# Router logits taken inside the layer-norm stage, with the norm's gain folded into the router's weights; sums of squares and parameter loads placed one stage earlier

## The reference

```python
x = _layernorm(DEEPNORM_ALPHA * x + mix, ln1_g[l], ln1_b[l])
ffn = _hier_moe(x, router_group_w[l], router_group_b[l], router_expert_w[l], ...)
x = _layernorm(DEEPNORM_ALPHA * x + ffn, ln2_g[l], ln2_b[l])

def _layernorm(x, g, b):            # (x - mean) / sqrt(var + 1e-5) * g + b
def _hier_moe(x, wg, bg, we, be, w_gate, w_up, w_down):
    glog = x @ wg + bg              # 4 group logits of each token
    elog = x @ we + be              # 16 expert logits of each token
    # best group, its two best experts, their weights; the experts' outputs are summed
```

```python
def rmsnorm(x, w):  return x * rsqrt(mean(x * x) + 1e-6) * w
```

## Time and profile before

| | us |
|---|---|
| median of 3 runs (2122.65 to 2130.05) | 2123.17 |
| profiled execution | 2123.46 |
| its span in the trace | 2121.3 |
| PE busy | 1743.2 (82%) |
| DVE busy | 1164.8 (55%) |
| ACT busy | 878.9 (41%) |
| POOL busy | 662.5 (31%) |

### The profile page before, as it was taken

One profiled execution on the slowest core, in us unless ns is written; L12 is line 12 of the kernel. 1 busy time (PEld: TensorE's weight loads), 2 busy tenths in 40 slices (PEclk: granted clock), 3 DMA queues, 4 the chain that ended last, 5 costly groups with the idle time before them and its releaser, 6 DMA issues. The chain is left out here.

```text
span 2121.3 us, 22435 instructions
## 1 busy us (share of the span) xinstructions
PE 1743.2 (82%) x7978; PEld 1347.0 (63%) x7978; DVE 1164.8 (55%) x1693; ACT 878.9 (41%) x1294; POOL 662.5 (31%) x348
## 2 busy tenths in 40 slices
PE   5999995859991799997666995499697689999997
PEld 4876532647870686742555884388367477888885
DVE  3926565649975564645556995592466414143241
ACT  2246555127872235655314884322645322111111
POOL 2337523101110333731401120144352023444441
PEclk8999987859995999997767997799889899999998
DMA  4201111057963311020117994320000122222221
GB/s 174 80 32 40 40 40 59 1 223 299 371 252 150 117 70 42 1 66 14 60 40 291 359 380 180 120 100 23 17 3 1 60 99 100 99 94 87 96 79 49
DMA packets 40476, 233.83 MB, mean 110 GB/s; under 512 B 9316, under 2 KB 9700, under 8 KB 20660
## 3 DMA queue, kind: packets, MB, share of 16 engines
q1 hardware_dynamic: 31012, 215.42, 26.9%
q0 software_dynamic: 9216, 16.80, 2.2%
q10 hardware_dynamic: 144, 0.26, 0.0%
HBM read 226.00 MB, written 23.23 MB: 117 GB/s over the span
## 5 line engine op out<-in xcount | busy, mean ns | idle before, releaser
L256 PE MATMUL bank<-XS,WS 128*128 128x512 f32 x864 | 201.9, 396 | 22.3 <-DVE WS L381 20.8
L2213 POOL TENSOR_TENSOR WS<-ring,WS 128x2048 fp32r<-128x2048 f32 x31 | 149.5, 4822 | 190.7 <-ACT WS L2205 190.7
L256 PEld LDWEIGHTS bank<-XS,WS 128*128 128x128 f32 x864 | 165.4, 192 | 58.4 <-DVE WS L381 21.3
L1235 PE MATMUL bank<-WS,XS 128*128 128x512 f32 x768 | 187.3, 400 | 1.1 <-DVE XS L1355 1.1
L2234 PE MATMUL bank<-XS,WS 128*128 128x512 f32 x768 | 174.9, 389 | 3.0 <-DVEq L2263 3.0
L2252 PE MATMUL bank<-WS,US 128*128 128x512 f32 x768 | 174.7, 389 | 0.0
L2205 ACT CAST WS<-ring 128x2048 fp32r<-128x2048 f32 x31 | 59.2, 1911 | 271.7 <-PE bank L2234 144.1
L1235 PEld LDWEIGHTS bank<-WS,XS 128*128 128x128 f32 x768 | 145.2, 193 | 31.3 <-DVE XS L1355 1.9
L2234 PEld LDWEIGHTS bank<-XS,WS 128*128 128x128 f32 x768 | 144.1, 188 | 33.1 <-DVEq L2263 3.2
L2252 PEld LDWEIGHTS bank<-WS,US 128*128 128x128 f32 x768 | 144.1, 188 | 29.9
L1572 PE MATMUL bank<-XS,WS 128*128 128x512 f32 (+1 forms) x600 | 136.4, 389 | 2.7 <-POOLq L1623 2.7
(11 more groups left out here) (487 smaller groups left out, 3534.8 us busy)
## 6 DMA issues: line engine op xcount, KB each, us to landing
raw<-in_w_exp SPq DMA_DIRECT2D x16, 2048.0 KB, 13.4
DN<-in_w_exp SPq DMA_DIRECT2D x32, 1024.0 KB
ring<-in_w_ff SPq DMA_DIRECT2D x32, 1024.0 KB, 4.7
raw<-in_w_in SPq DMA_DIRECT2D x20, 1024.0 KB, 4.8
GU<-in_w_exp SPq DMA_DIRECT2D x8, 2048.0 KB, 15.7
XT<-in_w_exp SPq DMA_DIRECT2D x8, 2048.0 KB, 16.1
ring<-in_w_in SPq DMA_DIRECT2D x12, 1024.0 KB, 4.8
raw<-in_w_out SPq DMA_DIRECT2D x8, 1024.0 KB, 5.0
```

The source lines that it names most:

```text
L256: last = pe.matmul(m.ps[g % 8][:, :], WS[:, i % 2, hw, at:at + P], XS[:, hx, k, :], start=(step == 0), stop=(step == 3 * KD - 1))
L1235: last = pe.matmul(m.ps[2 + e % 2][:, :], r.XS[:, e % 2, hx, 4 * half + k, :], r.WS[:, half, hw, k * S:(k + 1) * S], start=(half == 0 and ...
L2213: pool.tensor_tensor(f.WS[:, q % 2, 1, :], f.ring[:, q % 4, :], f.WS[:, q % 2, 0, :].bitcast(F32), ALU.subtract).then_inc(w_low, 1)
```

## The change

The second `transpose_stage` of a layer is gone, and so are the 32 logit matmuls of `router`. Both are now part of `norm_stage`, which works on the standardised tile before gain and bias: PE transposes each tile (`turn`), ACT copies the two banks to XT (`home`), PE makes the tile's logits with the folded weights WG = gain times WR as the stationary and XT as the moving operand (`logits_of`), ACT copies the 20 rows (`logits_back`) and PE transposes them back (`route`). The norm's bias enters through a row WB that is added to RP. DVE's gain and bias on X (`finish`) now wait until the tile has been transposed. At the stage's start the first weight quarter is cast in two halves, ahead of the chunks, and its low part is DVE's.

In the layer's first stage SP issues one weight chunk, then the parameters, then the other three chunks. In the second block the sums of squares of tiles 0 to 2 are taken at the end of the stage ahead (`combine_norm`, `out_projection_2`, `feed_forward`), and only that of tile 3 is left in `rms_transpose` and `final_norm` (which has the same lines as the diff shows of `rms_transpose`); `feed_forward` has the lines of `out_projection_2` with `summed` at 37 + t.

```diff
 def transpose_stage(nc, m, XS=None, loads=None, params=None):
-                loads(sp)
+                loads(sp, (0,))
             if params:
                 n = params(sp, param_in)
+            if loads:
+                loads(sp, (1, 2, 3))
...
 def norm_stage(nc, m, ln, layer, XS, WS):
         @block.tensor
         def _(pe):
...
+            def turn(t):
+                for half in range(2):
+                    pe.wait_ge(standard, 2 * t + half + 1)
+                    for k in range(4):
+                        last = pe.transpose(m.ps[2 * t + half][:, k * P:(k + 1) * P], m.X[:, t, (4 * half + k) * P:(4 * half + k + 1) * P], m.ident[:, :])
+                    last.then_inc(turned, 1)
+            def logits_of(t):
+                for k in range(KD):
+                    if k % 4 == 0:
+                        pe.wait_ge(xt_home, 2 * t + k // 4 + 1)
+                    last = pe.matmul(m.ps[2 * t][0:20, 0:P], ln.WG[:, k, :], m.XT[:, k, t * P:(t + 1) * P], start=(k == 0), stop=(k == KD - 1))
+                last.then_inc(logits, 1)
+            def route(t):
+                pe.wait_ge(logits_home, t + 1)
+                pe.transpose(m.ps[1][:, t * 20:(t + 1) * 20], ln.LT[0:20, t * P:(t + 1) * P], m.ident[0:20, 0:20]).then_inc(routed, 1)
...
+                        for k in range(4):
+                            if k % 2 == 0:
+                                pe.wait_ge(first_low, k // 2 + 1)
+                            pe.wait_ge(xt_low, k + 1)
...
+            for t in range(NT):
+                for half in range(2):
+                    pe.wait_ge(w_low, 2 + half)
+                    product(1, t, half).then_inc(tile_done, 1)
+                if t >= 1:
+                    turn(t - 1)
+                if t >= 2:
+                    logits_of(t - 2)
+                if t >= 3:
+                    route(t - 3)
+            logits_of(2)
+            route(1)
+            turn(3)
+            route(2)
+            logits_of(3)
+            route(3)
...
+        @block.scalar
+        def _(act):
...
+            first(0)
+            high(0)
+            high(1)
+            first(1)
+            high(2)
+            high(3)
+            weights(1)
+            for k in range(4, KD):
+                high(k)
+            weights(2)
+            weights(3)
+            standardise(0)
+            standardise(1)
+            home(0)
+            standardise(2)
+            home(1)
+            logits_back(0)
+            standardise(3)
+            home(2)
+            logits_back(1)
+            logits_back(2)
+            home(3)
+            logits_back(3)
...
+        @block.gpsimd
+        def _(pool):
+            for q in range(1, 4):
+                pool.wait_ge(w_high, q)
+                if q == 2:
+                    pool.wait_ge(xt_low, KD)
+                pool.tensor_tensor(WS[:, q, 1, :], m.raw[:, q, :], WS[:, q, 0, :].bitcast(F32), ALU.subtract).then_inc(w_low, 1)
...
         @block.vector
         def _(dve):
...
             def finish(t):
-                dve.wait_ge(standard, t + 1)
+                dve.wait_ge(turned, 2 * t + 2)
...
 def router(nc, m, r):
-            for t in range(NT):
-                for k in range(KD):
-                    last = pe.matmul(m.ps[0][:, t * 20:(t + 1) * 20], m.XT[:, k, t * P:(t + 1) * P], m.WR[:, k, :],
-                                     start=(k == 0), stop=(k == KD - 1))
-            last.then_inc(logits_done, 1)
...
 def combine_norm(nc, m, ln, r, layer):
+            def square(t):
+                act.wait_ge(finished, t + 1)
+                act.activation(r.MIX[:, t, 0:D], m.X[:, t, :], ACT.Square, accum_out=m.SS[:, t:t + 1]).then_inc(squared, 1)
...
+                if t >= 2:
+                    square(t - 2)
+            square(NT - 2)
+            act.wait_ge(squared, NT - 1)
...
 def rms_transpose(nc, m, n, XS, gain, first, extra=None):
-            for t in range(NT):
-                act.activation(n.XN[:, t, :], m.X[:, t, :], ACT.Square, accum_out=n.SS[:, t:t + 1]).then_inc(act_step, 1)
-            act.wait_ge(act_step, NT)
+            act.activation(n.XN, m.X[:, NT - 1, :], ACT.Square, accum_out=m.SS[:, NT - 1:NT]).then_inc(act_step, 1)
+            act.wait_ge(act_step, 1)
...
 def out_projection_2(nc, m, f):
+            for t in range(NT - 1):
+                act.wait_ge(summed, NT + t + 1)
+                act.activation(f.XQ, m.X[:, t, :].rearrange("p (a n) -> p a n", a=2), ACT.Square, accum_out=m.SS[:, t:t + 1]).then_inc(squared, 1)
+                act.wait_ge(squared, t + 1)
...
 def build(nc, d, out):
...
                         norm_stage(nc, m, ln, layer, XS, WS)
-                    transpose_stage(nc, m)
```

More of the change, by code:

```diff
@@ L962, in _, with product @@
         def _(pe):
-            if XS:
-                for kh in range(2):
-                    pe.wait_ge(xt_low, 4 * (kh + 1))
-                    for n in range(2 * NT):
-                        half, t = (n % 2, n // 2) if kh else (n // NT, n % NT)
-                        pe.wait_ge(w_low, 2 * kh + half + 1)
+            def product(kh, t, half):
+                step = 0
+                for k in range(4):
+                    for hw, hx in TERMS:
+                        last = pe.matmul(m.ps[2 * t + half][:, :], XS[:, hx, 4 * kh + k, t * P:(t + 1) * P], WS[:, 2 * kh + half, hw, k * S:(k + 1) * S],
+                                         start=(kh == 0 and step == 0), stop=(kh == 1 and step == 11))
+                        step += 1
+                return last
@@ L972, in _ @@
                         for k in range(4):
+                            if k % 2 == 0:
+                                pe.wait_ge(first_low, k // 2 + 1)
+                            pe.wait_ge(xt_low, k + 1)
                             for hw, hx in TERMS:
-                                last = pe.matmul(m.ps[2 * t + half][:, :], XS[:, hx, 4 * kh + k, t * P:(t + 1) * P], WS[:, 2 * kh + half, hw, k * S:(k + 1) * S],
-                                                 start=(kh == 0 and step == 0), stop=(kh == 1 and step == 11))
+                                pe.matmul(m.ps[0][:, :], XS[:, hx, k, 0:P], WS[:, 0, hw, k * S:(k + 1) * S], start=(step == 0), stop=False)
@@ L976, in _ @@
                                 step += 1
-                        if kh:
-                            last.then_inc(tile_done, 1)
+                        continue
+                    if half:
+                        pe.wait_ge(w_low, 1)
+                    if half and t == NT - 1:
+                        pe.wait_ge(weights_ready, 2)
+                    product(0, t, half)
+            pe.wait_ge(xt_low, KD)
+            for t in range(NT):
+                for half in range(2):
+                    pe.wait_ge(w_low, 2 + half)
[6 more added lines that the diff above has]
+                    route(t - 3)
@@ L993, in finish @@
                 link(dve.tensor_tensor(m.X[:, t, :], m.X[:, t, :], ln.GB[:, D:2 * D], ALU.add))
+            link(dve.tensor_tensor(ln.WG[:, :, :], m.WR[:, :, :], column(C_LB), ALU.mult))
+            dve.reduce_sum(ln.WB[:, :], ln.WG[:, :, :].rearrange("p k n -> p n k"), AX.X).then_inc(weights_ready, 1)
+            first(0)
+            low(0)
+            low(1)
+            first(1)
+            low(2)
+            low(3)
+            dve.wait_ge(weights_ready, 1)
+            link(dve.tensor_tensor(ln.WG[:, :, :], m.WR[:, :, :], column(C_LG), ALU.mult))
+            dve.wait_ge(bias_sum, 1)
+            dve.tensor_tensor(m.RP[:, R_RB:R_RB + 20], m.RP[:, R_RB:R_RB + 20], m.ps[7][:, 0:20], ALU.add).then_inc(weights_ready, 1)
+            for k in range(4, KD):
+                low(k)
             for t in range(NT):
@@ L2094, in out_projection_2 @@
 def out_projection_2(nc, m, f):
-    names = ("raw_in", "first_low", "w_high", "w_low", "xt_high", "xt_low", "block_done", "tile_done", "summed")
-    with stage(nc, "out_projection_2", *names) as (block, (raw_in, first_low, w_high, w_low, xt_high, xt_low, block_done, tile_done, summed)):
+    names = ("raw_in", "first_low", "w_high", "w_low", "xt_high", "xt_low", "block_done", "tile_done", "summed", "squared")
+    with stage(nc, "out_projection_2", *names) as (block, (raw_in, first_low, w_high, w_low, xt_high, xt_low, block_done, tile_done, summed, squared)):
         ORDER = (1, 0, 3, 2)
@@ L2205, in _ @@
                 act.copy(f.WS[:, q % 2, 0, :], f.ring[:, q % 4, :]).then_inc(w_high, 1)
+            for t in range(NT - 1):
+                act.wait_ge(summed, 37 + t)
+                act.activation(f.SQ[:, :, :].rearrange("p a n -> p (a n)"), m.X[:, t, :], ACT.Square, accum_out=m.SS[:, t:t + 1]).then_inc(final_squared, 1)
+                act.wait_ge(final_squared, t + 1)
         @block.gpsimd
@@ L2370, in build, with first_loads @@
                 one = bass.ds(layer, 1)
[L2372 to L2373 removed]
+                def first_loads(sp, chunks):
+                    for i in chunks:
```

137 lines of the change are left out of this document (74 added, 63 removed).

## The result

| | before | after |
|---|---|---|
| median of 4 runs, us | 2123.81 (2122.65 to 2130.05) | 2068.35 (2061.51 to 2071.16) |
| profiled execution | 2123.46 | 2069.1 |
| its span | 2121.3 | 2067.4 |
| PE, DVE, ACT, POOL busy | 1743.2, 1164.8, 878.9, 662.5 | 1734.3, 1138.7, 890.2, 652.5 |

The medians are 55.5 us apart. The ratio is 0.9728, interval 0.9698 to 0.9759, which is a gain of 51 to 64 us. PE lost 9 us of busy time and DVE 26: most of the gain is waiting, which the busy times do not show. The prediction was 2062, range 2054 to 2076.

What follows compares the result with a forecast made beforehand. Time was taken as a sum of barrier-ended stages, each set by what ends last. Norm stage and router 44.6, parameters 10.4, squares 2.2, 3.1 and 0.9 sum to 61.2 us, so 2123.5 - 61.2 = 2062, range 2054 to 2076.

Steps and rivals of the forecast that it cites:

- Start of the norm stage: Norm stage's start: PE's first product 3.0 us after the stage's start instead of 8.7, 5.7 us gained a layer.
- Added to PE: Norm stage: eight transposes 1.03 us, 16 logit records 1.73; 3.8 us ahead of the last tile's products, last product at 407.2.
- The tail: Norm stage behind the last product: router's first DVE step at 418.1 instead of 440.43, 22.3 us a layer, 44.6 in all.
- What the removed part cost: Between norm stage and router's first step: nothing but transposing and logits from 418.21 to 440.43, 22.2 us, each layer.
- Router's next bound: Router: SP's write of X, 7 us in all, stays hidden by 5 us behind DVE's routing of 12.4 us.
- Parameters: Layers' first stages: parameters ahead of three chunks land some 7.5 us earlier, before DVE ends; gain 5.0 + 5.4 = 10.4 us.
- Rival 3: First stages: early parameters do not land early, as their rows share engines with the chunks; 10.4 lost, 2073 us; chance 0.11.
- Squares: Second block, three of four squares moved a stage ahead: first rms_transpose 2.2 us, second 3.1, final_norm 0.9.
- Rival 1: Norm stage's start: DVE's fourth low part falls behind POOL's first (margin 0.5 us), PE stands 3.3 us a layer, 2069; chance 0.17.
- Rival 2: Norm stage's tail runs at 1.2 GHz after PE's pause: 2.3 us more a layer, 2067; chance 0.12.
- Rival 4: Experts: folded weights push one expert over 128 tokens, another pass of some 200 us, kernel ends at 2260; chance 0.02.
- The sum: Whole kernel: 44.6 + 10.4 + 2.2 + 3.1 + 0.9 = 61.2 us gained, 2062; as summed, chance 0.55.

Runs made afterwards that it cites:

- tail: Changed kernel with ACT's home(2) placed ahead of standardise(3): 2063.59 us, ratio 0.9729.
- params_only: Kernel before with one edit, parameters issued behind the first weight chunk: 2113.89 us against 2125.04, ratio 0.9948.
- norm_only: Kernel before with the norm stage and router of the changed one, parameters and squares as before: 2088.57 us, ratio 0.9821.
- slip: Changed kernel with two spare subtractions on DVE ahead of the fourth chunk's low part, so POOL's first starts first: 2077.54 us, ratio 0.9775.

## Why the prediction was right, point by point

- *Start of the norm stage*, 5.7 a layer: right in the place (PE at 3.06, forecast 3.0). Undone with the rest in place, it was worth 4.7.
- *Added to PE*: turn 1.03 as forecast; logits_of 1.92 where 1.73 was taken, in 16 records of 0.12. Last product at 399.5 - 346.9 = 52.6 us after the start; forecast 407.2 - 354.9 = 52.3.
- *The tail*: forecast from the last product to the router's first step 418.1 - 407.2 = 10.9, measured 411.04 - 399.5 = 11.5. The chain was the right one, through ACT's order; `tail` showed it by taking 1.8 to 2.4 out of it. Sum for this part: 21.3 and 20.7 a layer for 22.3. The step that was mis-sized is the logits' duration, which is exposed twice behind the last product and once ahead, 0.6 in all; the rest of the 1.0 to 1.6 I put down to small hand-overs between PE and ACT that were taken as nothing; no run separates them.
- *What the removed part cost*: 22.2 us was read off as the price of transposing and logits. The prediction did not see that some 5.8 of it came from half clock. It made no difference to the forecast, since the whole part went, but the same logits at full clock would have left less to gain.
- *Router's next bound*: covered, as forecast (router 12.34 and 12.18 to the experts).
- *Parameters*: 10.4 forecast, 10.2 in `params_only`, 11.1 by medians. In before WR was issued at 20.8 and landed 9.6 us later, at 30.4; now it is issued at 19.5 and lands 5.3 us later, at 24.8. That is 2.1 later than the 22.7 of the forecast and 0.9 ahead of DVE's end at 25.65: the gain is whole, since DVE is what ends last, but the margin is a third of what was worked out. Rival 3 did not happen.
- *Squares*: 2.2, 3.1, 0.9 forecast; 2.55, 3.2, 0.8 in the stages, and the FN row's DMA as releaser. The first of these came out near for a reason that the prediction did not give. It had DVE's low parts follow each other at 0.75 us from the end of the cast; in both traces the last copies and low parts wait for PE's transposing products, which end 1.5 us ahead of the last low part. These products start 3.1 us earlier (1.97 instead of 5.08 us into the stage) and end 2.9 earlier, and so the stage is shorter although the cast waits for its DMA as before. Combine_norm was put at nothing and was 1.2 and 0.5 shorter. In layer 1 up to 0.7 of that is chance (40.55 in `norm_only`, where it has no edit); in layer 2 the 0.5 shows in every profile with the edit.
- *Rival 1* did not happen, with 0.7 us to spare where 0.5 was forecast (seven DVE instructions stand ahead of the fourth chunk's, and not six as the text on the change says; the sum of the forecast has them right); `slip` shows that it is real and dearer than I said. The rule of the Trainium skill behind it ("SBUF — State Buffer", "SBUF: two separate sides": whoever has the shared ports keeps them for its instruction) agrees with both traces: 4.91 us for 0.65 in `slip`, and 4.60 in the earlier trace rows.
- *Rival 2* did not happen: granted clock 1.00 in the tail with pauses up to 1.69 us, and two groups of transposes and three of logits in it. The rule of the Trainium skill ("TensorE: Matmul & The Clock Gate", "Part 4: PE-mode transpose") made a cold tail likely; in this mix of transposes with logit matmuls the measurement decides against it. Transposes alone do not fit it either: in `params_only` 32 of them, behind a pause of 10.1 us, began at 0.50 and ended at 1.00. What keeps the clock up in the tail is not shown. That it is the logits can't be said, since the clock fell to 0.50 in the old form of them (128 columns stationary, 20 moving) while PE was busy.
- *Rival 4*: experts ran one pass.
- *The sum*: 61.2 forecast, 59.7 in the edited stages, 55.5 by medians. The interval of the ratio covers gains of 51 to 64 us, so the timings alone do not tell 61.2 from 55.5. Of the 59.7, 2.2 hang on the one profile of before whose layer 1 was slow between norm stage and experts; against the two others it is 57.5. What is left is no step that I can name: unedited stages vary by up to 12 us between profiles. The prediction had no term for that scatter, only a range that held it.

## What to carry to other kernels

In a program of stages with barriers, add up the stages that an edit touches, and compare them alone; a single total here carries 12 us of scatter from stages that nobody changed. Take more than one profile of the old code too: one touched stretch moved by 2.2 us between profiles with no edit in it. Look at the clock of the work that you are about to remove, for part of its price may not be its own. Work that waits at a stage's end may go behind the waits of the stage ahead, and there the order in which one engine's list is written (a copy ahead of the last tile's standardising instead of behind it) is worth microseconds. Where the order of two engines on a shared port rests on a margin below 1 us, force the slip once to know its price.

## What the runs showed of the hardware that was not expected

- The clock's return differs between executions of one program: behind the same pause of 4.73 us, full clock after 4 us in one profile and after 12 in another.
- In the experts' last unit, behind 3.0 us of pause, the mean clock was 0.50 to 0.70 in 21 of 22 units, and 1.00 in four of four with the pause filled to 0.45 us.
- The clock also fell while PE was busy: in the old logits (64 fp32 records, 128 columns stationary, 20 moving) from 1.00 to 0.50, within 4 us of their start, behind a pause of 1.72 us, in both layers of all three profiles that have them.
- A pause of PE cost more than its own length here: 4.34 us in `slip`, with 7.3 us of stage, the clock being 0.50 and then 0.74 over the 8 us behind it.
- An fp32 matmul with a stationary of 20 columns and 128 moving columns took two records of 0.12 us, against 0.108 for one with 128 columns of each, both at full clock: its 20 columns save nothing.
